# Unused matmuls at the residuals and in the diagonal stage are placed anew, and dt enters the decays' exponent as ln dt

## The chip, the core and the metric

The kernel runs on one core of a Trainium2 chip. The metric is the device time of one execution in microseconds. The core's engines are TensorE (PE; its weight loads are listed as PEld), VectorE (DVE), ScalarE (ACT), GpSimd (POOL) and SyncE (SP, which issues most transfers). PE's clock has two levels here, 1.2 and 2.4 GHz; the profile gives the granted share of the higher one.

## What is computed

A two-layer bidirectional encoder trunk, sequence 1024, width 1024, float32. Each sub-layer stands between RMS norms with shift, scale and gate from a conditioning vector:

```
for i in range(DEPTH):
    hm = rmsnorm(x, norm_g[i, 0]) * (1.0 + scale1) + shift1
    out = even_mixer(hm, ...) if i % 2 == 0 else odd_mixer(hm, ...)
    x = x + gate1 * rmsnorm(out, norm_g[i, 1])
    hf = rmsnorm(x, norm_g[i, 2]) * (1.0 + scale2) + shift2
    x = x + gate2 * rmsnorm(conv_glu(hf, ...), norm_g[i, 3])
```

The even mixer has a bidirectional state-space scan of 16 heads in chunks of 128 beside a pooling branch. The part of the scan that the change touches:

```
dt = softplus(dt_raw + dt_bias);  A = -exp(a_log)
xd = x * dt
a_cs = cumsum(dt * A, within a chunk);  Lmat = exp(a_cs[l] - a_cs[s]) where s <= l, else 0
y_diag[l] = sum over s of (C[l] . B[s]) * Lmat[l, s] * xd[s]
```

and the same backward; both directions and a skip term are added. The odd mixer is differential attention, and the last sub-layer of each layer is a gated convolutional feed-forward.

## The kernel before

Everything is kept transposed, features on partitions and the sequence along the free side, in 8 tiles of 128x1024. Matrix products run on PE with both operands split into a high and a low part (lines 218, 219 and 222). Each engine has its own program of stages in a fixed order, and semaphores join them; barriers stand around the first part of the scan, called ssd1 here, and around the diagonal stage.

In **ssd1** DVE computes dt (`dtS`) and dt*A (`aS`), PE sums it up within the chunks, DVE copies the cumulative sums (`csS`) out of PSUM, and ACT takes exponentials of them for the inter-chunk part (line 1168 on). `csb` is the bias that the decays' exponentials get: -cs for the forward, cs for the backward direction. ACT is idle between its copies of x (line 1162) and those exponentials.

The **diagonal stage** goes through 16 heads. For each head and direction (a group) PE writes the differences of the cumulative sums into `pG[:, d]`: four unused matmuls (line 1246), which the next ones overwrite, two that spread the head's row of sums (line 1249), two that add the mask (line 1253). ACT takes eight exponentials of it with `csb` as bias (line 1268). POOL multiplies the forward result by dt (line 1287), DVE the backward one (line 1299); DVE adds them (line 1304) and multiplies by the scores `Gm` (line 1308). PE multiplies the resulting weights by x (line 1237, `y_of`, three heads behind), and DVE adds the skip term as it evacuates (line 1294, four heads behind). PE may write a group's half of `pG` once the exponentials of the head before have read it. `E_` holds two heads, `W_` four.

At the **residuals** (e = 2, 4, 6, 8: after a mixer or a feed-forward), `residual` does on PE: the first shift product (`shift_pe`, not at e = 8), the sum of squares over partitions by one-column matmuls (`sums_pe`, line 271), after a square root on ACT and a reciprocal on DVE the spreading of the row factors (`rows_pe`, line 284), and the second shift product (line 312), which ACT must copy before it makes the first unnormed tile. DVE scales and adds the 8 tiles. `unnormed_pe` (line 333) then starts the next stage's first products from these tiles, one after the other; at e = 8 the output's transposes follow instead.

Of the kernel before, what the change touches and what calls it, by code (L numbers as in the profile page):

```python
# [61 lines left out]
def build(nc, io, out):  # L62
    ctx = ExitStack()
    with ctx:
# [3 lines left out]
        def at(name, kb, shape, dt=F32):  # L68
            return nc.alloc_sbuf_tensor_at(name, shape, dt, offset=base + int(kb * KB))
# [276 lines left out]
        def load_first(sp, e, u, srcs):  # L346
# [4 lines left out]
            for x in range(2):  # L351
                sp.dma_start(w_f[:, x, :].rearrange("p (k c) -> p k c", k=KT), srcs[x]).then_inc(s_wf, 16)

        def residual(who, eng, e, g, a=None, u=None):

            last = e == 8
            n = KT * (e // 2 - 1)
            if who == "pe":
                if e == 2:
                    eng.wait_ge(s_eva, 7)  # L360
                if not last:
                    shift_pe(eng, e, u, 0)
                eng.wait_ge(s_addV, add_v[e + 1])
                sums_pe(eng, sq_sum)
                rows_pe(eng, e)
                if not last:
                    shift_pe(eng, e, u, 1)
            elif who == "act":
                std_act(eng, e)
                if not last:  # L370
                    shift_act(eng, u)
                    for k in range(KT):
                        eng.wait_ge(s_resV, res_v(e, k))
                        eng.activation(Hf[:, k], X[:, k], ACT.Copy, scale=a(k)).then_inc(s_hf, 1)
                        eng.activation(O[:, k], X[:, k], ACT.Square).then_inc(s_sq, 1)
            elif who == "dve":
                rstd_dve(eng, e)
                for k in scale_dve(eng, e, O, g):
                    eng.wait_ge(s_t1, KT * e + k + 1)
                    eng.tensor_tensor(X[:, k], X[:, k], O[:, k], ALU.add).then_inc(s_resV, 1)  # L380
                if not last:
                    shift_dve(eng, e)
                    for k in range(1, KT):
                        if k > 1:
                            eng.wait_ge(s_addV, add_v[e + 1] + k - 1)
                        add_squares(eng, e + 1, 0, k, s_addV)
# [623 lines left out]
        def mods_dve(dve):  # L1010
# [17 lines left out]
            for n in range(len(SHIFTS)):  # L1028
# [25 lines left out]
        totS = at("tot_S", 74, [P, CH, 32])  # L1054
        arg = at("exp_args", 75, [P, 2, CH, 32])
        w0 = at("w0", 77, [P, CH, 32])
        E_ = at("decays", 32, [P, 2, 2, SEQ])
        W_ = at("chunk_weights", 48, [P, 4, SEQ])
        xw = at("x_w", AR + 32, [P, 2, 1024])
# [11 lines left out]
                                                  sem("cumsum_done"), sem("cumsum_copied"))  # L1071
        s_ex, s_T2h, s_T2l = (sem("decays_exp"), sem("cs_rows_hi"),
                                           sem("cs_rows_lo"))
        s_dif, s_exp, s_M, s_xd, s_y, s_yev = ([sem("diff0"), sem("diff1")], sem("exp_done"), sem("weights_done"),
                                               sem("forward_dt"), sem("y_done"), sem("y_evacuated"))
        s_sum = sem("directions_added")
        s_xw, s_Sp, s_st, s_off, s_tmp, s_yacc = ([sem("xw0"), sem("xw1")], [sem("S0"), sem("S1")],
                                                  [sem("st0"), sem("st1")], [sem("off0"), sem("off1")],
# [78 lines left out]
        def ssd1_act(act):  # L1157
            for c in range(CH):
                act.wait_ge(s_xst[c % 2], c // 2 + 1)
                if c == 0:  # L1160
                    act.wait_ge(s_xsp, X_OUT)
                act.activation(xS[:, c], pG[:, c % 2], ACT.Copy).then_inc(s_xsc[c % 2], 1)
                if c == 4:
                    act.wait_ge(s_sp, 2)
                    act.activation(sp_[:, 2], sp_[:, 1], ACT.Exp, scale=-1.0).then_inc(s_spe, 1)
                    act.activation(alog[:], alog[:], ACT.Exp).then_inc(s_spe, 1)
            act.wait_ge(s_csc, 7)
            act.activation(offE[:], arg[:, 0], ACT.Exp).then_inc(s_ex, 1)
            act.activation(w0[:], arg[:, 1], ACT.Exp).then_inc(s_ex, 1)
            act.activation(dec[:], totS[:], ACT.Exp).then_inc(s_ex, 1)  # L1170
            for g in range(2):
                act.wait_ge(s_bt, g + 3)
                act.activation(Gm[:, g], pM[:, g], ACT.Copy)
            act.wait_ge(s_cs2, 2)
            act.activation(T2[0:32, :], pG[0:32, 1], ACT.Copy).then_inc(s_T2h, 1)

        def ssd1_dve(dve):
# [25 lines left out]
            na = alog[:].rearrange("p (o h) -> p o h", o=1).to_broadcast([P, CH, 32])  # L1203
            then(dve.scalar_tensor_tensor(aS[:], dtS[:], -1.0, na, ALU.mult, ALU.mult))
            assert n[0] == 17, n
            dve.wait_ge(s_bt, 2)
            for h in range(2):
                dve.tensor_copy(BS[:, 4 * h:4 * h + 4].rearrange("p c n -> p (c n)"), pM[:, h]).then_inc(s_bc, 1)
# [9 lines left out]
            dve.tensor_tensor(arg[:, 0, :, b], totS[:, :, b], csS[:, :, b], ALU.subtract).then_inc(s_csc, 1)  # L1218
            dve.tensor_tensor(arg[:, 1, :, f], totS[:, :, f], csS[:, :, f], ALU.subtract).then_inc(s_csc, 1)
            dve.tensor_copy(arg[:, 1, :, b], csS[:, :, b]).then_inc(s_csc, 1)  # L1220
            dve.tensor_scalar(csb[:, :, f], csS[:, :, f], -1.0, None, ALU.mult).then_inc(s_csc, 1)
            dve.tensor_copy(csb[:, :, b], csS[:, :, b]).then_inc(s_csc, 1)
            dve.wait_ge(s_ex, 3)
            dve.tensor_tensor(wS[:], w0[:], dtS[:], ALU.mult).then_inc(s_csc, 1)
            dve.wait_ge(s_T2h, 1)
# [4 lines left out]
        def diag_pe(pe):  # L1230
            def y_of(h):
                if h >= 4:
                    pe.wait_ge(s_yev, h - 3)
                pe.wait_ge(s_M, h + 1)
                ps = pM[:, (h % 4) // 2, (h % 2) * HALF:(h % 2) * HALF + HALF]
                for c in range(CH):
                    last = pe.matmul(ps[:, c * 64:(c + 1) * 64], W_[:, h % 4, c * P:(c + 1) * P],
                                     xS[:, c, h * 64:(h + 1) * 64], start=True, stop=True)
                last.then_inc(s_y, 1)
            for h in range(SSM_HEADS):  # L1240
                for d in range(2):
                    hd = 16 * d + h
                    if h >= 1:
                        pe.wait_ge(s_exp, 2 * h - 1 + d)
                    for n in range(4):
                        pe.matmul(pG[:, d, n % 2 * HALF:(n % 2 + 1) * HALF], identR[:],  # L1246
                                  maskR[:, d:d + 1].to_broadcast([P, 4, P]), start=True, stop=True)
                    for n in range(2):
                        pe.matmul(pG[:, d, n * HALF:(n + 1) * HALF], selR[:, hd:hd + 1].to_broadcast([64, P]),
                                  T2[:, n * HALF:(n + 1) * HALF], start=True, stop=False)  # L1250
                    for n in range(2):
                        o = pG[:, d, n * HALF:(n + 1) * HALF]
                        last = pe.matmul(o, identR[:], maskR[:, d:d + 1].to_broadcast([P, 4, P]), start=False, stop=True)
                    last.then_inc(s_dif[d], 1)
                if h >= 3:
                    y_of(h - 3)
            y_of(SSM_HEADS - 3)
            y_of(SSM_HEADS - 2)
            y_of(SSM_HEADS - 1)

        def diag_act(act):
            for h in range(SSM_HEADS):
                for d in range(2):
                    if h >= 2:
                        act.wait_ge((s_sum, s_M)[d], (2 * h - 2, h - 1)[d])
                    act.wait_ge(s_dif[d], h + 1)
                    for c in range(CH):
                        last = act.activation(E_[:, h % 2, d, c * P:(c + 1) * P], pG[:, d, c * P:(c + 1) * P], ACT.Exp,
                                              bias=csb[:, c, 16 * d + h:16 * d + h + 1])
                    last.then_inc(s_exp, 1)  # L1270

        def by_chunk(ap):
            return ap.rearrange("p (c q) -> p c q", c=CH)

        def dt_of(d, h):
            return dtS[:, :, 16 * d + h:16 * d + h + 1].to_broadcast([P, CH, P])

        def diag_pool(pool):
            load_tiles(pool, yp_in, yp_dram)
            pool.wait_ge(s_fs, 16)  # L1280
            skew = bass.AP(tensor=f_dram.tensor, offset=P - 1, ap=[[2048, ATT_HEADS], [-1, P], [1, STRIP]])
            pool.dma_start(skew_dram, skew).then_inc(s_fs, 16)

            for h in range(SSM_HEADS):
                pool.wait_ge(s_exp, 2 * h + 1)
                e = by_chunk(E_[:, h % 2, 0])
                pool.tensor_tensor(e, e, dt_of(0, h), ALU.mult).then_inc(s_xd, 1)

        def diag_dve(dve):

# [4 lines left out]
                                         dskip[:, h:h + 1], ps, ALU.mult, ALU.add).then_inc(s_yev, 1)  # L1295
            for h in range(SSM_HEADS):
                dve.wait_ge(s_exp, 2 * h + 2)
                e = by_chunk(E_[:, h % 2, 1])
                dve.tensor_tensor(e, e, dt_of(1, h), ALU.mult).then_inc(s_sum, 1)
                if h >= 4:  # L1300
                    evac(h - 4)
                dve.wait_ge(s_sum, 2 * h + 1)
                dve.wait_ge(s_xd, h + 1)
                dve.tensor_tensor(E_[:, h % 2, 1], E_[:, h % 2, 1], E_[:, h % 2, 0], ALU.add).then_inc(s_sum, 1)
                dve.wait_ge(s_sum, 2 * h + 2)
                if h >= 4:
                    dve.wait_ge(s_y, h - 3)
                dve.tensor_tensor(W_[:, h % 4], E_[:, h % 2, 1], Gm[:, h // HPG], ALU.mult).then_inc(s_M, 1)
# [1064 lines left out]
```

## Time and profile before

| | |
|---|---|
| median of 3 runs | 3160.51 us (3157.14 to 3163.45) |
| the profiled execution | 3158.66 us, span 3156.3 us |
| mean granted PE clock | 0.969 |
| busy, share of the span | PE 95%, PEld 75%, DVE 55%, ACT 32%, POOL 8% |

The span runs from the first to the last instruction; the execution's own time holds a little more. Stages are found in the timeline by their lines; the diagonal stage lies from 514.7 to 623.6 us.

### The profile page before, as it was taken

How to read it: one execution, taken by the hardware profiler on the slowest of the kernel's cores; microseconds unless marked ns; L12 is line 12 of the kernel's file. 1: busy time of each engine (PE TensorE's matmuls, PEld its weight loads, DVE VectorE, ACT ScalarE, POOL GpSimd, SP SyncE). 2: the span in 40 equal slices, each digit the busy share in tenths (PEclk: the TensorE clock that was granted, in tenths of full speed). 3: DMA queues.
4: the chain of work that ended last, by engine and by line, in shares of the span. 5: the costliest groups of instructions: out<-in, count | busy, mean ns of one | idle time of the engine just before them, and what ended most of it. 6: DMA issues, size and time to landing. Idle time of an engine off the chain costs nothing.

```text
span 3156.3 us, 34192 instructions
## 1 busy us (share of the span) xinstructions
PE 2994.0 (95%) x13978; PEld 2376.5 (75%) x13978; DVE 1729.9 (55%) x2009; ACT 1016.6 (32%) x1481; POOL 237.9 (8%) x167
## 2 busy tenths in 40 slices
PE   6899998999989999999998999999799999999997
PEld 5667775666858788888875887878686878888886
DVE  7777775755484333333358776666738333333345
ACT  2213315612242121211234565555614112111122
POOL 2420002354000000000000000000000000000000
PEclk7999998999989999999999999999999999999998
DMA  5455473013411111111122111111121111111111
GB/s 201 141 174 166 148 253 136 34 47 114 147 41 54 47 47 54 47 47 47 47 78 80 32 41 42 51 40 55 56 97 39 47 47 47 47 53 43 50 47 60
DMA packets 270502, 240.22 MB, mean 76 GB/s; under 512 B 6877, under 2 KB 249022, under 8 KB 270334
## 3 DMA queue, kind: packets, MB, share of 16 engines
q1 hardware_dynamic: 257334, 185.61, 19.2%
q0 software_dynamic: 12000, 48.61, 4.1%
q10 hardware_dynamic: 1040, 4.19, 0.3%
q8 instruction: 92, 1.51, 0.2%
q14 instruction: 36, 0.29, 0.0%
HBM read 209.36 MB, written 36.90 MB: 78 GB/s over the span
## 4 chain that ended last, share of the span: by engine, by line
PE 76%; DVE 4%; ACT 2%; issue 1%; DMA 1%; POOL 0%; POOLq 0%; ACTq 0%; DVEq 0%
PE psum_gemm L218 11%; PE psum_gemm L219 11%; PE psum_gemm L222 11%; PE psum_gemm L1841 7%; PE psum_misc L218 7%; PE psum_misc L219 7%; PE psum_misc L222 7%; PE psum_gemm L333 3%; PE psum_misc L1905 3%; PE psum_gemm L1914 2%; PE psum_gemm L1926 2%; PE psum_gemm L1246 1%; PE psum_gemm L1353 1%; PE psum_gemm L1927 1%; DVE mix_out L300 1%
## 5 line engine op out<-in xcount | busy, mean ns | idle before, releaser
L218 PE MATMUL psum_gemm<-h_hi,w_hi 128*128 128x512 f32 x1968 | 779.3, 396 | 23.3 <-POOL h_lo L407 10.3
L219 PE MATMUL psum_gemm<-h_lo,w_hi 128*128 128x512 f32 x1968 | 767.9, 390 | 0.0
L222 PE MATMUL psum_gemm<-h_hi,w_lo 128*128 128x512 f32 x1968 | 607.5, 390 | 0.0
L218 PEld LDWEIGHTS psum_gemm<-h_hi,w_hi 128*128 128x128 f32 x1968 | 370.5, 188 | 123.7 <-issue 34.4
L219 PEld LDWEIGHTS psum_gemm<-h_lo,w_hi 128*128 128x128 f32 x1968 | 370.6, 188 | 77.7 <-issue 2.9
L222 PEld LDWEIGHTS psum_gemm<-h_hi,w_lo 128*128 128x128 f32 x1968 | 370.2, 188 | 77.9
L1626 ACT ACTIVATE w_hi<-w_raw 128x1024 fp32r<-128x1024 f32 x130 | 137.2, 1057 | 562.9 <-PE psum_misc L222 349.2
L218 PE MATMUL psum_misc<-ffn_act_hi,w_hi 128*128 128x512 f32 x704 | 275.7, 392 | 4.7 <-DVE ffn_act_lo L1734 4.7
L219 PE MATMUL psum_misc<-ffn_act_lo,w_hi 128*128 128x512 f32 x704 | 275.2, 391 | 0.0
L200 ACT ACTIVATE w_hi<-w_raw 128x1024 fp32r<-128x1024 f32 x79 | 83.2, 1056 | 484.5 <-PE psum_gemm L222 354.2
L1746 DVE TENSOR_TENSOR mix_out<-mix_out,psum_misc 128x1024 f32<-128x1024 f32 x80 | 97.7, 1221 | 231.3 <-PE psum_misc L222 231.3
L1712 DVE TENSOR_SCALAR gate_act<-gate_in,params 128x1024 f32<-128x1024 f32 x44 | 35.7, 812 | 334.8 <-ACT gate_in L1657 334.5
L222 PE MATMUL psum_misc<-ffn_act_hi,w_lo 128*128 128x512 f32 x704 | 217.7, 391 | 0.0
L205 DVE TENSOR_TENSOR w_lo<-w_raw,w_hi 128x1024 fp32r<-128x1024 f32 x79 | 105.6, 1339 | 136.2 <-ACT w_hi L200 136.2
L1730 DVE TENSOR_TENSOR gate_act<-gate_act,psum_gemm 128x1024 f32<-128x1024 f32 x42 | 51.3, 1221 | 204.1 <-PE psum_gemm L222 201.8
L1688 DVE TENSOR_TENSOR w_lo<-w_raw,w_hi 128x1024 fp32r<-128x1024 f32 x130 | 158.3, 1219 | 8.1 <-ACT w_hi L1626 8.1
L218 PEld LDWEIGHTS psum_misc<-ffn_act_hi,w_hi 128*128 128x128 f32 x704 | 133.1, 189 | 33.8 <-DVE ffn_act_lo L1734 5.6
L222 PEld LDWEIGHTS psum_misc<-ffn_act_hi,w_lo 128*128 128x128 f32 x704 | 132.7, 188 | 27.8
L219 PEld LDWEIGHTS psum_misc<-ffn_act_lo,w_hi 128*128 128x128 f32 x704 | 133.0, 189 | 27.3
L1657 ACT ACTIVATE gate_in<-psum_gemm 128x1024 f32<-128x1024 f32 x42 | 43.3, 1030 | 338.1 <-PE psum_gemm L222 338.1
L1841 PE MATMUL psum_gemm<-h_hi,w_hi 128*128 128x512 f32 x336 | 138.4, 412 | 6.3 <-ACT v_T L1980 3.8
L496 DVE SCALAR_TENSOR_TENSOR ada_w<-ada_w,silu_c 128x256 f32<-128x256 f32 x240 | 134.5, 560 | 8.6
(322 smaller groups left out, 4718.4 us busy)
## 6 DMA issues: line engine op xcount, KB each, us to landing
w_raw<-in_f_w_up SPq DMA_DIRECT2D x88, 512.0 KB, 3.8
ada_w<-in_w_ada SPq DMA_DIRECT2D x40, 1024.0 KB, 5.3
w_raw<-in_f_w_down SPq DMA_DIRECT2D x44, 512.0 KB, 3.4
w_raw<-in_e_w_in SPq DMA_DIRECT2D x29, 512.0 KB, 6.5
w_raw<-in_o_w_qkv SPq DMA_DIRECT2D x24, 512.0 KB, 3.9
ada_w_first<-in_w_ada SPq DMA_DIRECT2D x4, 2048.0 KB, 19.6
w_raw<-in_e_w_out SPq DMA_DIRECT2D x16, 512.0 KB, 4.1
skew_scratch<-bias_scratch POOLq DMA_DIRECT2D x1, 7680.0 KB, 49.5
```

Source lines behind the costliest of these rows:

```text
L200: act.activation(w_hi[:, s], w_raw[:, s], ACT.Copy).then_inc(s_hi, 1)
L205: dve.tensor_tensor(w_lo[:, s], w_raw[:, s], w_hi[:, s].bitcast(F32), ALU.subtract).then_inc(s_lo, 1)
L218: pe.matmul(o, wh, rh[:, k, c], start=(k == 0), stop=False)
L219: pe.matmul(o, wh, rl[:, k, c], start=False, stop=False)
L222: last = pe.matmul(o, wl, rh[:, k, c], start=False, stop=(k == nk - 1))
L333: mm = pe.matmul(dst(x)[:, c], w_f[:, x, k * P:(k + 1) * P], Hf[:, k, c], start=(k == 0), stop=(k == KT - 1))
L496: dve.scalar_tensor_tensor(w[:, 0], w[:, k], c, w[:, 0], ALU.mult, ALU.add).then_inc(s_avc, 1)
L1626: act.activation(w_hi[:, s], w_raw[:, s], ACT.Copy).then_inc(s_hi, 1)
L1688: dve.tensor_tensor(w_lo[:, s], w_raw[:, s], w_hi[:, s].bitcast(F32), ALU.subtract).then_inc(s_lo, 1)
L1746: dve.tensor_tensor(O[:, t], O[:, t], pM[:, t % 2], ALU.add).then_inc(s_dev[t % 2], 1)
L1841: mm = pe.matmul(ps, w, (Hh, Hl, Hh)[x][:, k, c], start=(i == 0), stop=(i == 23))
L1905: mm = pe.matmul(pM[:, m, n * HALF:(n + 1) * HALF], q[r, b * P:(b + 1) * P], k[r, n * HALF:(n + 1) * HALF], start=(x == 0), stop=(x == 2))
```

## The change

- In the diagonal stage a group gets eight unused matmuls in heads 0 and 1 and one from head 2 on, where it had four.
- dt is no longer multiplied into the exponentials. ACT takes ln of dt (held above 1e-37) once in ssd1, and DVE adds it to `csb`, so that exp(difference + csb) holds dt. The products on POOL and DVE and their semaphores go; ACT's waits are renumbered.
- At each residual PE issues unused matmuls of 512 columns: eight before the sums, three before the row factors, and, but at e = 8, six before the second shift product. They write a half of PSUM that nothing reads.

```
+        def keep_clock_pe(pe, e, n):
+
+            o = (pM if e == 2 else pG)[:, 1, HALF:]
+            for _ in range(n):
+                pe.matmul(o, Hh[:, 0, 0:P], Hh[:, 0, 0:HALF], start=True, stop=True)
+
...
                 if not last:
                     shift_pe(eng, e, u, 0)
+                keep_clock_pe(eng, e, 8)
                 eng.wait_ge(s_addV, add_v[e + 1])
                 sums_pe(eng, sq_sum)
+                keep_clock_pe(eng, e, 3)
                 rows_pe(eng, e)
                 if not last:
+                    keep_clock_pe(eng, e, 6)
                     shift_pe(eng, e, u, 1)
...
+        lnd = at("ln_dt", 78, [P, CH, 32])
...
+            act.wait_ge(s_lndt, 1)
+            act.activation(lnd[:], lnd[:], ACT.Ln).then_inc(s_lndt, 1)
             act.wait_ge(s_csc, 7)
             act.activation(offE[:], arg[:, 0], ACT.Exp).then_inc(s_ex, 1)
...
             assert n[0] == 17, n
+            dve.tensor_scalar(lnd[:], dtS[:], 1e-37, None, ALU.max).then_inc(s_lndt, 1)
             dve.wait_ge(s_bt, 2)
...
-            dve.tensor_scalar(csb[:, :, f], csS[:, :, f], -1.0, None, ALU.mult).then_inc(s_csc, 1)
-            dve.tensor_copy(csb[:, :, b], csS[:, :, b]).then_inc(s_csc, 1)
+            dve.wait_ge(s_lndt, 2)
+            dve.scalar_tensor_tensor(csb[:, :, f], csS[:, :, f], -1.0, lnd[:, :, f], ALU.mult, ALU.add).then_inc(s_csc, 1)
+            dve.tensor_tensor(csb[:, :, b], csS[:, :, b], lnd[:, :, b], ALU.add).then_inc(s_csc, 1)
...
-                    for n in range(4):
+                    for n in range(8 if h < 2 else 1):
                         pe.matmul(pG[:, d, n % 2 * HALF:(n % 2 + 1) * HALF], identR[:],
                                   maskR[:, d:d + 1].to_broadcast([P, 4, P]), start=True, stop=True)
...
                     if h >= 2:
-                        act.wait_ge((s_sum, s_M)[d], (2 * h - 2, h - 1)[d])
+                        act.wait_ge((s_sum, s_M)[d], h - 1)
...
-            for h in range(SSM_HEADS):
-                pool.wait_ge(s_exp, 2 * h + 1)
-                e = by_chunk(E_[:, h % 2, 0])
-                pool.tensor_tensor(e, e, dt_of(0, h), ALU.mult).then_inc(s_xd, 1)
...
                 dve.wait_ge(s_exp, 2 * h + 2)
-                e = by_chunk(E_[:, h % 2, 1])
-                dve.tensor_tensor(e, e, dt_of(1, h), ALU.mult).then_inc(s_sum, 1)
+                dve.tensor_tensor(E_[:, h % 2, 1], E_[:, h % 2, 1], E_[:, h % 2, 0], ALU.add).then_inc(s_sum, 1)
                 if h >= 4:
                     evac(h - 4)
-                dve.wait_ge(s_sum, 2 * h + 1)
-                dve.wait_ge(s_xd, h + 1)
-                dve.tensor_tensor(E_[:, h % 2, 1], E_[:, h % 2, 1], E_[:, h % 2, 0], ALU.add).then_inc(s_sum, 1)
-                dve.wait_ge(s_sum, 2 * h + 2)
+                dve.wait_ge(s_sum, h + 1)
```

## Rows read from the trace of the kernel before

**Rows 1.** The page: busy us, share of the span and instructions of each engine.
```profile
PE 2994.0 (95%) x13978; PEld 2376.5 (75%) x13978; DVE 1729.9 (55%) x2009; ACT 1016.6 (32%) x1481; POOL 237.9 (8%) x167
```

**Rows 2.** Windows, diagonal stage: length, PE, PEld, DVE, ACT, POOL busy, clock, DMA.
```profile
514.70:525.30 10.60, 10.60 (x22) 6.00 (x22) 0.25 (x1) 4.35 (x16) 4.68 (x4) 0.52 0.82 307
541.00:603.70 62.70, 62.70 (x321) 44.71 (x320) 42.90 (x41) 43.57 (x160) 20.13 (x10) 1.00 0.19 81
```

**Rows 3.** Groups by line, 514 to 630: busy us, mean ns, idle before.
```profile
L1299 DVE TENSOR_TENSOR decays<-decays,dt_S 128x1024 f32<-128x1024 f32 x16 | 20.2, 1262 | 36.9 <-ACT decays L1268 36.9
```

**Rows 4.** Timeline of one steady head (head 9): start us, us, what, idle before.
```profile
570.93 1.18 PE L1246 MATMUL psum_gemm<-mask_r,ident_r 128*128 128x512 f32 x4
...
573.27 1.08 PE L1246 MATMUL psum_gemm<-mask_r,ident_r 128*128 128x512 f32 x4
...
573.53 4.41 ACT L1268 ACTIVATE decays<-psum_gemm,exp_bias 128x128 f32<-128x128 f32 x16 [1.86 <-PE psum_gemm L1253]
...
574.28 0.72 PE L1249 MATMUL psum_gemm<-cs_rows,sel_r 64*128 64x512 f32 x2
...
574.93 0.73 PE L1253 MATMUL psum_gemm<-mask_r,ident_r 128*128 128x512 f32 x2
...
575.50 1.89 PE L1237 MATMUL psum_misc<-x_S,chunk_weights 128*128 128x64 f32 x16
```

**Rows 5.** Timeline of the first heads, PE and ACT (heads 0, 2, 4).
```profile
518.52 1.91 PE L1246 MATMUL psum_gemm<-mask_r,ident_r 128*128 128x512 f32 x4
...
522.53 1.91 PE L1246 MATMUL psum_gemm<-mask_r,ident_r 128*128 128x512 f32 x4
...
522.77 2.18 ACT L1268 ACTIVATE decays<-psum_gemm,exp_bias 128x128 f32<-128x128 f32 x8 [1.77 <-PE psum_gemm L1253]
...
531.07 4.43 ACT L1268 ACTIVATE decays<-psum_gemm,exp_bias 128x128 f32<-128x128 f32 x16 [0.41 <-PE psum_gemm L1253]
...
542.19 3.12 ACT L1268 ACTIVATE decays<-psum_gemm,exp_bias 128x128 f32<-128x128 f32 x11 [1.86 <-PE psum_gemm L1253]
```

**Rows 6.** Timeline of the last head (15) and the stage's end.
```profile
611.13 4.41 ACT L1268 ACTIVATE decays<-psum_gemm,exp_bias 128x128 f32<-128x128 f32 x16 [1.73 <-PE psum_gemm L1253]
...
619.99 2.80 PE L1237 MATMUL psum_misc<-x_S,chunk_weights 128*128 128x64 f32 x16 [1.43 <-DVE chunk_weights L1308]
```

**Rows 7.** Timeline of ssd1 (DVE, ACT), and of a table load before a wait.
```profile
504.05 0.42 DVE L1204 SCALAR_TENSOR_TENSOR a_S<-dt_S,a_log 128x256 f32<-128x256 f32 x1
...
508.42 0.42 ACT L1168 ACTIVATE off_decay<-exp_args 128x256 f32<-128x256 f32 x1 [8.04 <-DVE exp_args L1220]
...
797.18 1.28 ACT L290 ACT_TABLE_LOAD   x1
799.08 0.27 ACT L290 ACTIVATE std<-psum_misc,eps 128x8 f32<-128x8 f32 x1 [0.62 <-PE psum_misc L271]
```

**Rows 8.** Windows of the slow stretch at residuals e = 2, 4, 8.
```profile
873.50:890.60 17.10, 14.60 (x53) 12.23 (x54) 9.11 (x11) 5.53 (x8) 0.00 (x0) 0.50 0.44 114
1631.30:1645.00 13.70, 11.72 (x43) 9.69 (x44) 8.02 (x8) 4.85 (x7) 0.00 (x0) 0.50 0.65 212
3122.90:3140.00 17.10, 12.41 (x54) 10.84 (x54) 11.20 (x11) 3.35 (x4) 0.00 (x0) 0.50 0.12 43
```

**Rows 9.** Residual e = 2 (slow), the next norm (fast); windows of the unnormed matmuls.
```profile
873.95 3.57 PE L271 MATMUL psum_misc<-ones,square_sum 128*128 128x1 f32 x16 [3.25 <-DVE square_sum L256]
...
878.18 3.78 PE L284 MATMUL psum_misc<-ident,rstd 128*128 128x128 f32 x16 [0.66 <-DVE rstd L294]
...
912.66 1.84 PE L271 MATMUL psum_misc<-ones,mix_out 128*128 128x1 f32 x16
...
916.16 1.95 PE L284 MATMUL psum_misc<-ident,rstd 128*128 128x128 f32 x16
...
886.00:890.60 4.60, 4.04 (x5) 1.85 (x6) 4.57 (x4) 4.46 (x6) 0.00 (x0) 0.50 0.00 0
894.00:906.00 12.00, 12.00 (x29) 5.32 (x28) 11.79 (x12) 10.30 (x11) 0.00 (x0) 1.00 0.01 1
```

More of the change, by code:

```diff
@@ L1073, in build @@
                                            sem("cs_rows_lo"))
-        s_dif, s_exp, s_M, s_xd, s_y, s_yev = ([sem("diff0"), sem("diff1")], sem("exp_done"), sem("weights_done"),
-                                               sem("forward_dt"), sem("y_done"), sem("y_evacuated"))
+        s_dif, s_exp, s_M, s_lndt, s_y, s_yev = ([sem("diff0"), sem("diff1")], sem("exp_done"), sem("weights_done"),
+                                               sem("ln_dt_steps"), sem("y_done"), sem("y_evacuated"))
         s_sum = sem("directions_added")
@@ L1270, in diag_act @@
                     last.then_inc(s_exp, 1)
[L1272 to L1276, printed above, removed]
         def diag_pool(pool):
```

## Prediction

> **What bounds the kernel.** I read the page first. TensorE (PE) is busy for 95% of the span of 3156.3 us [rows 1], so a change counts where PE does work that could go, where PE stands, or where it runs at the lower of its two clocks. The execution took 3158.66 us, 2.4 us around its span. The median of the three runs is 3160.51, so the sum below is made against 3158.66 and the forecast moved up by 1.9.
>
> Then I asked for the stretches around the two edits. In the diagonal stage the granted clock is 0.52 (almost all at 1.2 GHz) from 514.7 to 525.3, and 1.00 (2.4 GHz) from 541.0 to 603.7, where PE is busy for all of 62.70 us while ACT, the engine of the exponentials, is busy for 43.57, DVE for 42.90 and POOL for 20.13 [rows 2]. So past the first heads PE sets the pace, not the vector engines from which the two dt products are taken. The timeline confirms it: ACT idles 1.86 us before every head's exponentials, waiting for PE, and from head 4 (542.19) to head 15 (611.13) a head takes 68.94/11 = 6.27 us [rows 4 to 6].
>
> At the residuals the clock is 0.50 for 17.1, 13.7, 17.1 and 17.1 us (e = 6, not shown, as e = 2) [rows 8], though PE is busy for 14.60 us of the first: it is busy with narrow matmuls, the norm's sums (one column each), the row factors and the shift products (two columns) [rows 9]. Being busy with these did not bring the clock back; only the wide matmuls behind them did. This matters for the change, whose unused matmuls are 512 wide.
>
> **Diagonal stage, steady heads.** A group (one head, one direction) is now four unused, two row and two mask matmuls. The four take 573.27 to 574.28 = 1.01 us, the two row ones 0.65, the two mask ones 0.57; the group before takes 573.27-570.93 = 2.34, this one 2.23, and the y product the rest of 6.27, which is 1.70 [rows 4]. Four cost 1.01 where two of the same form cost 0.57, so one more costs 0.22. The change takes three from each group: 2 x 3 x 0.22 = 1.32 us, so PE needs 4.95 us a head. The next limit is ACT, 4.41 us a head [rows 4]; PE still binds. Eleven head periods: 11 x 1.32 = 14.5 us saved. Bounds: 0.25 a matmul (1.01/4) makes it 16.6; ACT's 4.41 is the floor, 11 x 1.86 = 20.5.
>
> **The two dt products.** In the steady heads they cost nothing today: POOL's (20.13/10 = 2.0 us [rows 2]) and DVE's (1.26 [rows 3]) lie beside a PE that is never free. The one on DVE stands on the end once: after the last exponential (611.13 + 4.41 = 615.54 [rows 6]) come DVE's product of 1.2 us, an evacuation, the sum and the weights, then at 619.99 PE's last y product [rows 6]. That product goes: 1.2 us saved. POOL only loses work.
>
> **First heads.** Heads 0 and 1 get eight unused matmuls a group: 16 more. In the slow stretch a group of eight takes 522.53-518.52 = 4.01 us [rows 5], 0.50 a matmul against 2.23/8 = 0.28 at the higher clock; one more costs twice 0.22 there, four 1.7 us. If the clock rises where it does now, 525.3, the first two groups cost 3.4 more and the next two 1.8 more; that puts head 2's first exponential 3.5 us later than 531.07. Heads 2 and 3 then go at ACT's 4.4 instead of 4.84, and head 4 starts 1.8 us later than 542.19. If the longer unbroken run of full-height matmuls brings the clock up one or two groups sooner, each group behind it takes about 1.7 us less, and head 4 starts 0.8 us earlier. I take the middle, 0.5 us lost, which includes the next item.
>
> **The logarithm.** DVE gains one small operation (128x256, a quarter of the 1.26 us product [rows 3]) ahead of B's copies, which PE waits for: 0.3 us. The two exponent operations become two-input ones, under 0.1 us longer, behind what ACT waits for; they are hidden by DVE's own wait for ACT. ACT gains the logarithm (about 0.4) and, since the table with the exponential doesn't stay, two table loads of 1.28 us. ACT is idle for 8.04 us before 508.42 [rows 7]. At L290 a load ran at 797.18 while its activation waited until 799.08 for PE, so a load does not wait for its activation's input [rows 7]. The first load starts at 500.4; its input is there 0.3 us after dt*A, which DVE ends at 504.47 [rows 7]; the logarithm is through by 505.3, the second load by 506.6, under the 508.75 or so at which the exponential is due: cost 0. Without that cover the two loads and the logarithm would cost 3.0. The Trainium skill prices a switch higher: ScalarE: Activation LUTs, section What ACT_TABLE_LOAD costs, has about 1.28 us for the load and a drain of about 1.38 behind it. The trace agrees on the load; the drain isn't seen at L290. An estimate with the page's sum ends the second switch near 508.0, still hidden; if both loads also waited for their inputs, it would end near 510.5 and cost 1.8 us.
>
> Diagonal stage in all: 14.5 + 1.2 - 0.5 = 15.2 us saved.
>
> **Residuals.** Eight unused matmuls stand before the sums, three before the row factors, six before the second shift product. If they kept the clock at 2.4 GHz throughout: the sums take 1.84 instead of 3.57 us, the rows 1.95 instead of 3.78, each of these measured at both clocks [rows 9]. Both are on the chain: sums, standard deviation, reciprocal, rows, scale, residual, first unnormed tile. That is 3.5 us. The second shift product, sixteen narrow matmuls as the sums are, gains the same 1.7, and the six unused ones in front of it cost 6 x 0.22 = 1.3: 0.4 saved, on the path, as ACT's copy of it stands ahead of the first unnormed tile. The unnormed matmuls that follow are slow for 4.0 us, at 0.86 a record where they later take 0.43 [rows 9]: 2.0 saved. So 5.9 at the first and third residual, 1.7 less at the second (its slow stretch is 3.4 us shorter), 3.5 at most at the last: 19.5. The first eight cost 1.8 us and fit into PE's idle time (3.25 before the sums of the first residual [rows 9]); the three cost 0.66, just the 0.66 in which PE waits for the reciprocal [rows 9].
>
> I don't believe the whole. After the eight there is 1.5 us of idle time and 1.8 of one-column sums, and after the six another 1.9 of two-column products and 1.3 of waiting for the unnormed tile: two stretches per residual in which PE does nothing wide, and narrow work kept it slow before. Where it falls, the unused ones run at 0.43 each: three then cost 1.3 in a gap of 0.66, six cost 2.6 in front of the shift. With everything slow as now, the change would lose 0.6 + 2.6 at three residuals and 0.6 at the last: 10.2 lost. The clock is at 2.4 GHz when the eight start, so the sums and part of the rows should be won at most of them. I take 9 us saved, half of the full sum.
>
> **Sum.** 15.2 + 9 = 24.2 us: 3158.7 - 24.2 = 3134.5, and 3136.4 beside the median. I forecast 3136 us.
>
> **The rivals.**
> (a) The unused matmuls at the residuals don't hold the clock and their gain and loss cancel: 15 us saved, 3145. For it: the narrow stretches above. Against: the clock falls now only after 3 us without wide work. Chance 0.2.
> (b) PE's issue gaps shrink too, ACT's 4.41 us becomes the pace (6.0 us more) and the residuals give 15: 36 saved, 3124. Chance 0.08.
> (c) The other sign: with fewer matmuls PE has pauses in the diagonal stage and the clock falls to 1.2 GHz there. A group of five then takes 4.01 [rows 5] less 3 x 0.43 = 2.7, the y product 2.8 (the last one, in part slow [rows 6]): 8.2 us a head against 6.27. Eleven heads: 21 lost instead of 14.5 won, total 11 slower, 3172. It decides once about two thirds of those heads run slow. Against it: PE would be busy for all of 4.95 us a head, and even the stretch 541 to 603.7 with its small y products holds 1.00 [rows 2]. Chance 0.05. The Trainium skill, TensorE: Matmul & The Clock Gate, section A second HAM failure mode, tells of such pauses between groups of matmuls that throttle the array again and again; no row of the stretch 541 to 603.7 shows it so far, and removing filler is what would bring it on.
> (d) The table loads and the narrow gaps at the residuals all go wrong (3 and 10 lost): 2 us saved, 3158. Chance 0.05.
>
> **How the numbers follow.** Forecast as summed, 0.62; (a) 0.2, (b) 0.08, (c) 0.05, (d) 0.05. The forecast's own range is 3129 to 3143: residuals 3 to 16, first heads 2.6 wide, steady heads 14.5 to 16.6. The range for 8 in 10 takes in (a) and ends short of (b)'s extreme: 3125 to 3149. A difference of 0.2% is 6.3 us, about what a measurement of this kernel can tell. Faster: forecast, (a), (b) and a little of (d): 0.91; same 0.04; slower 0.05.
>
> **What would show it.** Steady heads at about 4.95 us between exponentials, ACT's idle before them near 0.5, PE still full and its clock 1.00; if the period is 4.4 the price of a removed matmul was too low. The logarithm and both loads inside ACT's idle time before the decay exponentials. Head 4 within 2 us of 542. At each residual, the sums at 1.8 us and the rows near 2.0 if the clock held, and slow stretches shorter than 17.1 us. The prediction is wrong if the clock falls between heads, if the sums and rows stay at 3.6 and 3.8, or if the second shift product comes later than now and carries the first unnormed tile with it.

## The result and the profile after

The changed kernel takes 3129.28 us (median of 4, 3123.81 to 3133.12) against 3158.82 before: ratio 0.9907, 95% interval 0.9887 to 0.9927, so 29.5 us or 0.93% faster. The forecast was 3136 us with a range of 3125 to 3149. The profiled execution took 3133.12 us, its span is 3131.4: 24.9 us under the span of before. A second measurement of the same kernel (e5 below) gave 3130.74 us and 0.9906 (0.9892 to 0.9920).

The page after: PE's share of the span is as before [rows 1], and it is busy for 11 us less.

```profile
span 3131.4 us, 34135 instructions
...
PE 2982.7 (95%) x13972; PEld 2367.7 (76%) x13972; DVE 1709.0 (55%) x1994; ACT 1018.0 (33%) x1484; POOL 205.6 (7%) x151
```

Where the 24.9 us of the two spans come from is read off at marks that both programs pass; each line is the start of the named work.

| mark | before | after | apart |
|---|---|---|---|
| first exponential of the diagonal stage | 518.8 | 520.1 | +1.3 |
| head 4's exponentials | 542.2 | 541.1 | -1.1 |
| head 15's exponentials | 611.1 | 594.8 | -16.3 |
| first work behind the stage's barrier | 623.7 | 605.1 | -18.6 |
| sums at e = 2 | 874.0 | 856.3 | -17.7 |
| row factors of the norm behind it | 916.2 | 893.1 | -23.1 |
| sums at e = 4 | 1630.1 | 1605.5 | -24.6 |
| row factors behind it | 1670.9 | 1643.8 | -27.1 |
| sums at e = 6 | 2365.7 | 2342.1 | -23.6 |
| row factors behind it | 2407.8 | 2383.2 | -24.6 |
| sums at e = 8 | 3121.8 | 3097.6 | -24.2 |
| end | 3156.3 | 3131.4 | -24.9 |

Up to the barrier behind the diagonal stage 18.6 us are won, and at the four residuals 5.4, 2.5, 1.0 and 0.7, together 9.6. The stretches with unchanged work in between differ by 1.5 us won to 3.5 lost; the 3.5 lie in the attention, where the clock was low for longer than before.

A steady head, from the timeline of PE and ACT (start us, us, what):

```profile
544.10 0.47 PE L1260 MATMUL psum_gemm<-mask_r,ident_r 128*128 128x512 f32 x1
544.50 0.72 PE L1263 MATMUL psum_gemm<-cs_rows,sel_r 64*128 64x512 f32 x2
545.15 0.73 PE L1267 MATMUL psum_gemm<-mask_r,ident_r 128*128 128x512 f32 x2
...
545.72 0.39 PE L1260 MATMUL psum_gemm<-mask_r,ident_r 128*128 128x512 f32 x1
545.98 4.24 ACT L1282 ACTIVATE decays<-psum_gemm,exp_bias 128x128 f32<-128x128 f32 x16 [0.63 <-PE psum_gemm L1267]
546.04 0.72 PE L1263 MATMUL psum_gemm<-cs_rows,sel_r 64*128 64x512 f32 x2
546.69 0.73 PE L1267 MATMUL psum_gemm<-mask_r,ident_r 128*128 128x512 f32 x2
547.26 1.90 PE L1251 MATMUL psum_misc<-x_S,chunk_weights 128*128 128x64 f32 x16
...
550.85 4.24 ACT L1282 ACTIVATE decays<-psum_gemm,exp_bias 128x128 f32<-128x128 f32 x16 [0.63 <-PE psum_gemm L1267]
```

The groups take 1.62 and 1.54 us where [rows 4] have 2.34 and 2.23, ACT waits 0.63 us for PE instead of 1.86, and a head takes 4.87 us. The windows say the same for the eleven heads: PE busy for all of 53.80 us at the full clock, DVE down to 32.22, where ten heads took 42.90 before [rows 2].

```profile
516.50:541.00 24.50, 23.24 (x90) 14.23 (x90) 8.37 (x7) 17.00 (x64) 2.77 (x3) 1.00 0.70 270
541.00:594.80 53.80, 53.80 (x288) 37.68 (x286) 32.22 (x33) 46.69 (x176) 0.00 (x0) 1.00 0.25 102
```

The first of these windows differs from before at its start: the clock is at 1.00 from the stage's first matmul on, where [rows 2] had 0.52 until 525.3.

ssd1, ACT's timeline: both table loads and the logarithm lie in its idle time, and ACT still waits 2.07 us for DVE before the first exponential (8.04 in [rows 7]).

```profile
500.40 1.28 ACT L1178 ACT_TABLE_LOAD   x1
504.92 0.42 ACT L1178 ACTIVATE ln_dt<-ln_dt 128x256 f32<-128x256 f32 x1 [3.24 <-DVE ln_dt L1218]
505.36 1.28 ACT L1180 ACT_TABLE_LOAD   x1
508.71 0.42 ACT L1180 ACTIVATE off_decay<-exp_args 128x256 f32<-128x256 f32 x1 [2.07 <-DVE exp_args L1233]
```

The residual e = 2 in the timeline, to set beside [rows 9]: the sums take 1.95 us instead of 3.57, the row factors 2.05 instead of 3.78, and the unused matmuls are L358.

```profile
852.89 2.11 PE L358 MATMUL psum_misc<-h_hi 128*128 128x512 f32 x8
...
856.28 1.95 PE L271 MATMUL psum_misc<-ones,square_sum 128*128 128x1 f32 x16 [1.28 <-DVE square_sum L256]
858.09 0.94 PE L358 MATMUL psum_misc<-h_hi 128*128 128x512 f32 x3
...
858.89 2.05 PE L284 MATMUL psum_misc<-ident,rstd 128*128 128x128 f32 x16
860.70 1.62 PE L358 MATMUL psum_misc<-h_hi 128*128 128x512 f32 x6
...
864.03 0.17 ACT L319 ACTIVATE shift_product<-psum_gemm 128x4 f32<-128x4 f32 x1 [5.50 <-PE psum_gemm L312]
```

The windows from the sums to the first unnormed matmul at e = 2, 4, 6 (and to the scale at e = 8) give the clock, the third number from the end: 1.00, 0.84, 0.79, 0.72, where [rows 8] have 0.50. The clock held through one residual and fell inside the other three, at the end of the sums or behind them.

```profile
856.30:865.40 9.10, 7.71 (x58) 7.07 (x58) 4.55 (x5) 1.63 (x4) 0.00 (x0) 1.00 0.80 206
1605.50:1616.10 10.60, 9.21 (x58) 8.61 (x58) 5.64 (x6) 2.46 (x5) 0.00 (x0) 0.84 0.96 313
2342.10:2352.80 10.70, 9.29 (x58) 8.71 (x58) 4.58 (x5) 1.63 (x4) 0.00 (x0) 0.79 0.53 133
3097.60:3103.80 6.20, 6.14 (x35) 5.66 (x35) 0.22 (x2) 0.27 (x1) 0.00 (x0) 0.72 0.00 0
```

### The profile page after: what moved, and what is told of

Same layout as the page of the kernel before. It is cut to its first block, busy times and chain, and to the rows that moved or that the text cites. A ratio compares the mean times of both kernels' runs of the same rounds, so it can differ in the third digit from the quotient of the medians.

```text
span 3131.4 us, 34135 instructions
## 1 busy us (share of the span) xinstructions
PE 2982.7 (95%) x13972; PEld 2367.7 (76%) x13972; DVE 1709.0 (55%) x1994; ACT 1018.0 (33%) x1484; POOL 205.6 (7%) x151
## 4 chain that ended last, share of the span: by engine, by line
PE 77%; DVE 4%; ACT 2%; issue 1%; DMA 0%; POOL 0%; POOLq 0%; ACTq 0%; DVEq 0%
PE psum_gemm L218 11%; PE psum_gemm L219 11%; PE psum_gemm L222 11%; PE psum_gemm L1840 7%; PE psum_misc L218 7%; PE psum_misc L219 7%; PE psum_misc L222 7%; PE psum_gemm L333 3%; PE psum_misc L1904 3%; PE psum_gemm L1925 2%; PE psum_gemm L1913 2%; PE psum_gemm L1926 1%; PE psum_gemm L1352 1%; DVE mix_out L300 1%; PE psum_misc L1342 1%
```

## The experiments

The theory: in the diagonal stage PE's own work sets the pace, so the fewer unused matmuls bring nearly all and the logarithm only the end of the stage; at the residuals the wide unused matmuls keep the clock up for part of the way. The rivals: the dt products on POOL and DVE count as well; the gain lies in where the clock's slow stretches happen to fall. Times are medians; "before" is run beside each batch.

**The halves of the change.** e1 leaves the residual calls out, e2 puts them alone into the kernel before.

```
# e1, in residual()
-                keep_clock_pe(eng, e, 8)
-                keep_clock_pe(eng, e, 3)
-                    keep_clock_pe(eng, e, 6)
# e2: the kernel before with keep_clock_pe and these three calls
```

> The changed kernel without its unused matmuls at the residuals; the diagonal stage and the logarithm as changed. If the two edits are worth what the two traces show apart (18.5 us up to the end of the diagonal stage, 6.4 behind it), this kernel is 18 to 19 us faster than before, with slow stretches of 13 to 17 us back at each residual, sums at 3.2 to 3.6 us. If instead the residual edit is worth nothing and the shorter residuals come from other phases of the clock, it is as fast as the changed kernel, 25 us and more under before.

> The kernel before with the unused matmuls at the residuals alone. If they hold the clock through sums and rows, each residual from its sums to the next norm's rows is 1 to 5 us shorter, 9 to 10 us over the four, and the kernel is 0.3% faster. The rival: where the clock falls all the same they cost time, gain and loss cancel, and the time is within 3 us of before.

e1 took 3147.47 us against 3158.39, ratio 0.9962 (0.9948 to 0.9977): 11 us faster, where 18 to 19 were expected. e2 took 3152.07, ratio 0.9976 (0.9967 to 0.9986): 6.3 us faster, a third less than the 9 to 10 expected, and not zero. In e1's trace the stage itself is as in the changed kernel: from the first exponential to the sums at e = 2 it is 337.4 us, after 336.2, before 355.1, so 18 us shorter. But its first exponential came at 523.6 (before 518.8), and its attention took 3.5 us more than before. Of the 4.8 us at the start, 3.5 lie ahead of the stage's first matmul, where only the logarithm's operations are new; the other 1.3 lie in the first group, which has four more unused matmuls. Its four residuals took what they took before, within 0.3 us. In e2's trace the residuals are worth 1.0, 2.5, 3.8 and -0.7 us, 6.5 together.

**The halves of the diagonal edit.** e3 changes the counts of unused matmuls alone, e4 brings the logarithm alone (four unused matmuls throughout, none at the residuals).

```
# e3: the kernel before with
-                    for n in range(4):
+                    for n in range(8 if h < 2 else 1):
# e4: the changed kernel without the residual calls, with
-                    for n in range(8 if h < 2 else 1):
+                    for n in range(4):
```

> The kernel before with the new counts of unused matmuls in the diagonal stage alone: eight a group in heads 0 and 1, one from head 2 on; dt is still multiplied on POOL and DVE. If PE's work sets the pace, a steady head takes 4.9 us as in the changed kernel, and the stage ends only 1 to 2 us later than there: 16 to 18 us faster than before. The rival: with PE shorter, the four DVE operations of a head (4.4 us busy) and POOL's product behind the exponentials become the pace, a head takes 5.3 us or more, and under 11 us of the gain is left.

> The kernel before with the logarithm alone: four unused matmuls a group as before, none at the residuals, the dt products gone. If PE's work sets the pace, a head stays at 6.27 us and only the 1.2 us at the stage's end are won, 0.3 lost ahead of it: within 2 us of before. The rival, that the products held the heads up: a head gets shorter than 6.0 us, and 4 us or more are won.

e4: 3157.72 us, ratio 0.9998 (0.9989 to 1.0008), a steady head at 6.27 us, as expected. e3: 3154.34 us, ratio 0.9985 (0.9977 to 0.9994), only 4 us faster; a head takes 5.28 us, and the rival was right. These runs and e1 stand beside the same runs of the kernel before, so they can be set against each other: the counts alone give 4 us, the logarithm alone 1, both 11. ACT, DVE and POOL of one head of e3 (timeline):

```profile
575.57 1.22 DVE L1299 TENSOR_TENSOR decays<-decays,dt_S 128x1024 f32<-128x1024 f32 x1
576.68 1.92 POOL L1287 TENSOR_TENSOR decays<-decays,dt_S 128x1024 f32<-128x1024 f32 x1 [3.37 <-ACT decays L1268]
576.70 0.74 DVE L1294 SCALAR_TENSOR_TENSOR y_S<-x_S,d_skip,psum_misc 128x512 f32<-128x512 f32 x1
577.36 2.32 DVE L1304 TENSOR_TENSOR decays<-decays 128x1024 f32<-128x1024 f32 x1
579.71 1.22 DVE L1308 TENSOR_TENSOR chunk_weights<-decays,G_scores 128x1024 f32<-128x1024 f32 x1
579.72 4.25 ACT L1268 ACTIVATE decays<-psum_gemm,exp_bias 128x128 f32<-128x128 f32 x16 [1.04 <-DVE decays L1304]
```

ACT now waits for DVE, not for PE, and DVE never pauses: its four operations fill the head, and a window shows it busy for 54.62 of 55.00 us.

```profile
545.00:600.00 55.00, 53.78 (x275) 35.83 (x273) 54.62 (x42) 44.42 (x168) 21.05 (x11) 1.00 0.19 80
```

The sum of the directions (L1304) takes 2.32 us here (2.82 and 2.90 in two earlier heads, the figure of the next text) and 1.22 in the kernel before. POOL's product ends at 578.60, 1.24 us after the sum began; the sum is longer by 1.10. The evacuation (L1294), which ran beside the same product and reads one of its operands from PSUM, kept its 0.74. Two edits of e3 ask whether that is the cause.

```
# e9: POOL's product on 8 columns, one of each chunk
-                pool.tensor_tensor(e, e, dt_of(0, h), ALU.mult)...
+                pool.tensor_tensor(e[:, :, 0:1], e[:, :, 0:1], dt_of(0, h)[:, :, 0:1], ALU.mult)...
# e10: the same cut in DVE's product instead
```

> The fillers-only kernel (8 and 1 unused matmuls, no logarithm, nothing at the residuals) with POOL's dt product cut from 1024 to 8 columns a head, one of each chunk; DVE's stays whole. The forward direction then lacks most of its dt. There DVE's sum of the directions took 2.9 us a head instead of 1.2 while POOL's product ran, and a head took 5.28 us. If it is POOL's work beside DVE that stretches the sum, the sum is back at 1.2 us and a head takes PE's 4.88. If it is the length of DVE's own chain, a head stays near 5.3.

> The same, with DVE's dt product cut to 8 columns instead and POOL's whole; the backward direction then lacks most of its dt. If POOL's work stretches whatever DVE does beside it, one DVE operation a head still takes about 2.9 us, but DVE has 1.2 us less to do, and a head takes between 4.88 and 5.1 us. If the length of DVE's chain alone counts, 4.88 with no operation stretched.

Both give 4.88 us a head (one execution each: 3145.65 and 3148.47 us against 3158.53). In e9 DVE keeps all four operations and each is back at its usual length, 4.42 us in all:

```profile
576.98 1.23 DVE L1299 TENSOR_TENSOR decays<-decays,dt_S 128x1024 f32<-128x1024 f32 x1 [0.61 <-ACT decays L1268]
577.59 4.25 ACT L1268 ACTIVATE decays<-psum_gemm,exp_bias 128x128 f32<-128x128 f32 x16 [0.64 <-PE psum_gemm L1253]
578.12 0.74 DVE L1294 SCALAR_TENSOR_TENSOR y_S<-x_S,d_skip,psum_misc 128x512 f32<-128x512 f32 x1
578.78 1.22 DVE L1304 TENSOR_TENSOR decays<-decays 128x1024 f32<-128x1024 f32 x1
...
580.04 1.23 DVE L1308 TENSOR_TENSOR chunk_weights<-decays,G_scores 128x1024 f32<-128x1024 f32 x1
```

So DVE's chain alone does not hold the head at 5.28; POOL's product beside DVE's sum, which reads two SBUF operands, does. In e10 POOL works at full length, but for 1.66 of its 2.13 us in a pause of DVE, and no operation of DVE is stretched:

```profile
572.08 2.13 POOL L1287 TENSOR_TENSOR decays<-decays,dt_S 128x1024 f32<-128x1024 f32 x1 [2.75 <-ACT decays L1268]
...
574.10 0.18 DVE L1299 TENSOR_TENSOR decays<-decays,dt_S 128x8 f32<-128x8 f32 x1 [1.66 <-ACT decays L1268]
...
574.85 1.22 DVE L1304 TENSOR_TENSOR decays<-decays 128x1024 f32<-128x1024 f32 x1
```

So it takes both: POOL's whole product, and a DVE without the pause that the product used to fall into. The Trainium skill names this contention in GPSIMD Engine Reference, section Specifications: GpSimd's SBUF interfaces are shared with VectorE, with contention against DVE instructions that have two SBUF inputs. The trace agrees, with 2.32 against 1.22 us.

**The counts of unused matmuls.** Three edits of one line of the changed kernel:

```
-                    for n in range(8 if h < 2 else 1):
+                    for n in range(8 if h < 2 else 0):      # e6
+                    for n in range(4 if h < 2 else 1):      # e7
+                    for n in range(8 if h < 2 else 2):      # e11
```

> The changed kernel with no unused matmul from head 2 on, where it has one a group. If a head costs what PE has to do, it goes from 4.88 to about 4.45 us, which is ACT's own 4.4: 4 to 5 us faster than the changed kernel. The rival: PE now pauses between the groups, the clock falls to 1.2 GHz in the stage, a head takes 7 us or more and the kernel is 20 us slower or worse.

> The changed kernel with four unused matmuls a group in heads 0 and 1 instead of eight. If the eight bring the clock up early, the clock now stays at 1.2 GHz for 10 us into the stage and head 4 starts no earlier than 541 us, no gain from the 16 matmuls left out. If the early rise was only where the clock happened to stand, head 4 starts 2 to 4 us sooner and the kernel is that much faster.

> The changed kernel with two unused matmuls a group from head 2 on instead of one. At 0.22 to 0.25 us a matmul a head goes from 4.88 to 5.3 us, the stage gets 5 us longer, and the kernel is 5 us slower than the changed one, in all its runs at the higher clock. If PE no longer sets the pace, nothing is lost.

e11: 3138.13 us, ratio 0.9942 (0.9928 to 0.9955), 7.4 us slower than e5, which was measured in another batch; by the two traces the eleven heads are 5.2 us longer, as expected. A head takes 5.35 us against 4.88, so a matmul costs 0.24; PE sets the pace at one and at two.

e6: 3180.69 us, ratio 1.0069 (1.0056 to 1.0081): 21 us slower than before and 50 slower than the changed kernel. All six executions are long (3177.7 to 3186.8). The rival was right about the clock and the time. The windows of its trace: the clock is 1.00 until 531.9, where PE has just stood for 0.94 us in head 2, and 0.50 from there to the end of the stage. Whether the pauses or the fewer wide matmuls as such brought it down was not separated.

```profile
511.40:531.90 20.50, 17.13 (x74) 11.09 (x73) 4.33 (x4) 11.50 (x39) 2.77 (x3) 1.00 0.65 234
531.90:640.00 108.10, 107.92 (x334) 77.90 (x334) 43.96 (x44) 59.94 (x222) 0.00 (x0) 0.50 0.16 68
```

A head takes 7.91 us there. Note that PE is busy for 107.92 of 108.10 us and the clock does not come back: the slower clock makes PE look full.

e7: its seven executions fall into two groups, 3127.84, 3133.32 and 3134.49 us, and 3186.78, 3194.40, 3195.73 and 3196.16. The time alone does not say why, so the trace of a long one (3196.16) is read: the clock falls at 516.7, as the stage begins, and stays at 0.50 for 153.6 us.

```profile
503.00:516.70 13.70, 9.04 (x50) 7.58 (x50) 7.62 (x18) 5.67 (x8) 0.82 (x2) 0.75 0.01 1
516.70:660.00 143.30, 143.30 (x417) 99.42 (x416) 48.18 (x47) 69.46 (x256) 1.95 (x2) 0.50 0.21 85
```

A head takes 8.87 us. In the kernel before the clock fell at the same place (515.1) and was back at 525.3; there every group had four unused matmuls. In e1, e3, e8, e10 and e11, with eight in the first heads, it fell between 515.8 and 519.2 and was back after 6.8 us each time (after 3.4 in e9). In e7's long execution heads 0 and 1 are the same as in the kernel before, but 14.3 us after the fall, when PE reaches head 2 at 531.0, the clock is still down, and with one unused matmul a group it does not come back for the rest of the stage. So four a group leave it open whether the clock is up in time; in each of the six traces where it fell with eight it was. No trace of a short execution of e7 was taken, but the mean granted clock of each execution was taken: 0.950 to 0.953 for the four long ones, 0.972, 0.972 and 0.975 for the three short ones, as for the changed kernel (0.972 to 0.977 in nine). So the short ones did not spend the stage at the lower clock.

The fall at the stage's start is itself not always there, and four unused matmuls a group do not decide it: the clock stayed up in the profiled execution, e5, e6 and e12 with eight, and in e4 with four. e1's window and e4's:

```profile
518.20:525.90 7.70, 7.70 (x19) 5.19 (x20) 0.00 (x0) 2.18 (x8) 2.78 (x3) 0.56 0.74 255
515.20:538.50 23.30, 23.08 (x90) 13.79 (x91) 9.15 (x8) 17.38 (x65) 2.77 (x3) 1.00 0.72 274
```

**The changed kernel and its diagonal half again.**

> The changed kernel once more, for its interval beside the two kernels with half of the change: the diagonal half alone took 0.38% off and the residual half alone 0.24%. If the halves simply add, this is 18 to 20 us under before; the first measurement had 29. If it stays near 29, about 10 us belong to neither half alone.

> The changed kernel without the unused matmuls at the residuals, once more. By the traces the diagonal half is worth 18 us from the first exponentials to the first residual, but its first measurement was only 11 under before. If that lay in where the clock's slow stretches fell before and behind the stage in those runs, it now comes out 14 to 20 under before; if it stays at 11, the whole change is worth more than its halves and the traces have not shown why.

e5: 3130.74 us (0.9906). e12: 3143.19 us against 3158.53, ratio 0.9960 (0.9946 to 0.9973), 15 us faster. e12's trace passes the first exponential at 518.9 and the sums at e = 2 at 855.1; e5's at 518.2 and 854.4. From there to the end e5 is 10.4 us shorter: by 3.6, 3.4, 3.5 and 1.5 us at the residuals, 12.1 together, and 1.7 lost between them. So both halves are there: 11 and 15 us for the diagonal half in two measurements, 18 to 19 from the first exponential to e = 2 by their traces.

**The six moved behind the shift product.**

```
-                    keep_clock_pe(eng, e, 6)
                     shift_pe(eng, e, u, 1)
+                    keep_clock_behind(eng, e)     # two float32 matmuls of 512 columns, ident by ident
```

> The changed kernel with the six unused matmuls at the residuals e = 2, 4, 6 taken from in front of the second shift product, and two 512-column float32 ones (as long as four records, 1.7 us) put behind it, where PE waits for the first unnormed tile. If the six stand on the path, the first unnormed tile comes 0.7 us sooner after the row factors at each of the three residuals (the residual's own addition is next), 2 us in all, and the clock holds as well. The rival: without them the shift product is a longer narrow stretch, the clock falls there and the first unnormed matmuls run at 1.2 GHz, 2 us lost at each.

3134.52 us (3120.79 to 3139.56), ratio 0.9911 (0.9893 to 0.9929): not to be told from e5. The six do stand on the path. From the end of the row factors to the first unnormed matmul it is 3.90, 3.90 and 3.91 us in e8's trace at e = 2, 4 and 6, where the changed kernel has 4.45, 4.45 and 4.47: 0.55 us sooner each time, near the 0.7 expected. The ends at e = 4, the changed kernel first:

```profile
1608.53 3.11 PE L284 MATMUL psum_misc<-ident,rstd 128*128 128x128 f32 x16
...
1616.09 2.38 PE L333 MATMUL psum_gemm<-h_unnormed,w_first 128*128 128x512 f32 x5 [1.39 <-ACT h_unnormed L383]
...
1612.50 2.01 PE L284 MATMUL psum_misc<-ident,rstd 128*128 128x128 f32 x16
...
1618.41 4.10 PE L333 MATMUL psum_gemm<-h_unnormed,w_first 128*128 128x512 f32 x9 [0.40 <-ACT h_unnormed L389]
```

But the clock decides more than the place of the six. From the sums to the next norm's row factors e8 takes 37.6 us at e = 4, where the clock held up to the next norm (38.3 in the changed kernel), and 39.2 and 40.0 at e = 2 and 6, where it fell at the row factors; the changed kernel had 36.8 and 41.1 there in one trace and 38.4 and 38.3 in the other. No version tried beats the changed kernel clearly.

## Why the prediction was right, and where it was not

**The steady heads.** Forecast: 14.5 us from 1.32 a head, PE still the pace. Measured: head 4 to head 15 takes 53.7 us instead of 68.9, 15.2 less, 1.38 a head. A matmul was priced at 0.22 and costs 0.23 to 0.24 (e11). The claim that PE sets the pace holds, for before (e4) and after (e11).

**The dt products.** Forecast: worth 1.2 us at the stage's end and nothing in a steady head, ACT's 4.41 us being the next limit. This step was wrong. It is true only of the kernel before, as e4 shows. With PE's work cut, the next limit with the products in place is DVE at 5.28 us a head, above PE's 4.88 and ACT's 4.41. In e3's trace the eleven heads save 10.8 us and not 15.2, and 7.4 us are won up to the barrier, where the changed kernel has 18.6. Part of that distance is the clock's: it was low from 608.6 to 622.2 in e3 and from 604.0 to 610.9 in the changed kernel. The sum came out right because the change does both, so that the products are gone when PE's work is cut: by medians the logarithm is worth 1 us without the fewer matmuls and 7 with them. In the working I asked what hides the products and not what they would cost with that cover gone. DVE's load per head alone would not have shown it: 42.90 us for ten heads [rows 2] is 4.29 a head, under PE's 4.95, and e9 runs at 4.88 with all four DVE operations. POOL's product lengthening DVE's sum stood in no row of the steady heads, since it ran in a pause of DVE (1.99 us before the product L1299) that the shorter heads no longer have.

**The first heads and the logarithm.** Forecast: 0.5 us lost. Measured up to head 4: 1.1 won, and that was luck with the clock. From the stage's first matmul to head 4's exponentials it is 27.5 us before and 27.6 in e1, e3, e8 and e10, where the clock fell and eight brought it back after 6.8 us instead of 10.2 (26.1 in e9, where it was back after 3.4). It is 24.6 in the profiled execution, e5 and e12, and 23.4 in e4 with four, all with the clock up. So up to head 4 the new counts gain nothing where the clock falls and cost 1.2 us where it does not. What the eight give is a clock that is up before head 2, from where one a group holds it; e7's long executions are what happens otherwise. In the working, heads 2 and 3 are both said to take 4.84 us before; head 3 took 6.28, and only with that does 3.5 us later at head 2 become 1.8 at head 4. Ahead of the stage its first matmul comes 1.9 us later than before: DVE's small operation costs 0.2 (from dt*A's start to the first exponential of ssd1 4.58 us against 4.37; forecast 0.3), and the slow stretch in ssd1 lasts 6.8 us (505.0 to 511.8) and not 3.4. The loads and the logarithm on ACT cost nothing, as forecast.

**The end of the stage.** Forecast 1.2 us won, measured 2.2 (from the last exponentials' start to the work behind the barrier 12.5 and 10.3 us). Besides DVE's product, the last y product took 2.03 us and not 2.80 [rows 6], as the clock fell 1.8 us into it and before had fallen 0.9 us into it.

**The residuals.** Forecast: 9 us, half of what a held clock would give, with a range of 3 to 16. Measured: 9.6 in the profiled execution, 6.5 in e2, 12.1 in e5 against e12. At e = 2 with the clock up throughout, 5.4 us against the 5.9 worked out. The reason given for taking half, that narrow stretches remain and the clock falls in some, is what the traces show. In the seven traces with these unused matmuls the clock stayed up at the start of the sums every time. It then held up to the first unnormed matmul at e = 2 in three of them (the profiled execution, e5 and e11), at e = 4 only in e8, and at e = 6 and e = 8 in none. The working counted on a clock that falls only after 3 us without wide work; at e = 4 it fell 2.2 us after the eight, with PE busy nearly all the time.

**The other sign, (c).** It did not happen in nine executions of the changed kernel, whose mean granted clock is 0.972 to 0.977. But the case is real and near: one unused matmul less a group and it happens every time (7.91 us a head, the forecast's estimate was 8.2), four less in the first heads and it happens in four of seven. The forecast's reason against it, that PE would be busy for all of 4.95 us a head, was not a good one, since PE is also full while the clock is down.

**What stays open.** The whole change is worth 29 us by medians; the two halves give 11 and 15 (e1, e12) and 6.3 (e2), 17 to 22. By the traces the halves are 18 to 19 from the first exponential to e = 2, and 6.5 to 12 at the residuals. What e1's trace lacks is lost ahead of the stage (first exponential between 517.5 and 523.6 in the fourteen traces), in the stage's first group and in the attention; but the changed kernel's profiled execution lost the same 3.5 us in the attention. Why the clock's slow stretches fall where they do, and why the whole is worth more than its halves, was not settled. Nor was it settled what decides the clock's fall at the stage's start, on which e7's two groups may hang: with the logarithm it was absent in five of nine traces, without it in none of five.

## What to carry to other kernels

Before costing an edit at nothing because another engine is busy longer, recompute every engine's load per round with the other edits of the same change in place, and look which operations then run side by side; here two edits were worth 4 and 1 us alone and 11 together. Matmuls that do nothing are worth their time only as long as the clock stands on them, so try one more and one fewer and take several executions: at one fewer this kernel lost 50 us, and at a smaller start its time split in two groups. A gain that hangs on the clock should be read stage by stage, between marks that both kernels pass and at the same clock, as the total moves by several microseconds with slow stretches in work that nobody touched.

## What the runs showed of the hardware

- A stage can lock itself at 1.2 GHz: PE busy for 143.30 of 143.30 us at a granted clock of 0.50 (e7), with 512-column matmuls among 64-column ones, while the same instructions at 1.00 kept the clock there for 53.80 us (after).
- A DVE sum of two SBUF operands took 2.32 us instead of 1.22 while POOL's product of 128x1024 ran beside it for 1.24 us, and 1.22 with that product cut to 8 columns (e3, e9): the overlap was added almost whole. An operation of DVE with one operand in SBUF and one in PSUM kept its 0.74 us beside the same product.
- A table load was run while its activation still waited for its input: it ended at 501.68, the logarithm came at 504.92 (after).
- The clock can fall while PE is busy: at e = 4 it fell at 1607.5, and PE had been busy for all but 0.13 us since 1603.26, with eight matmuls of 512 columns (2.11 us) and then sixteen of one (1.95 us) (after).
